# A decoder-layer step in fp32: input and first weight tile in halves, woven; squares of two norms added on VectorE; the root applied to the query tiles

## The reference, cut to what matters

```python
def decoder_layer(x, ...):
    y, ... = head_group_mixer(rms_norm(x, g_mix), ...)    # xn @ w_in (1024 -> 2048), convs, RG-LRU scan, @ w_out
    x = x + y
    x = x + cross_attention(rms_norm(x, g_xa), mem_k, mem_v, w_q, w_o)
    x = x + routed_experts(rms_norm(x, g_moe), moe_w)     # top 4 of 32 experts
    return x, ...
def rms_norm(x, g):
    return x * rsqrt(mean(x * x, axis=-1) + EPS) * g
def cross_attention(xn, k, v, w_q, w_o):
    q = xn @ w_q                                           # 4 heads of 256
    p = softmax(einsum('bthd,bmhd->bhtm', q, k) * 256 ** -0.5)
    return einsum('bhtm,bmhd->bthd', p, v) @ w_o
```

## Time and profile before

| | |
|---|---|
| time, median of 3 runs | 1243.32 us (1242.83 to 1243.99) |
| span of the profiled execution, first to last instruction | 1243.5 us |
| PE busy | 1161.0 us (93%), 5560 matmuls |
| PE weight loads busy | 569.9 us (46%) |
| DVE busy | 331.2 us (27%) |
| ACT busy | 183.6 us (15%) |
| DMA moved | 457.45 MB, 368 GB/s over the span |

### The profile page before, as it was taken

The page is one execution under the profiler, slowest core; times in us unless marked ns, Lnnn a source line. Parts: engine busy times, 40 slices in busy tenths (PEclk is TensorE's granted clock), DMA queues, the critical chain, the costliest instruction groups (busy, mean ns, idle before and its releaser), DMA issues.

```text
span 1243.5 us, 14380 instructions
## 1 busy us (share of the span) xinstructions
PE 1161.0 (93%) x5560; PEld 569.9 (46%) x5560; DVE 331.2 (27%) x799; ACT 183.6 (15%) x357; POOL 44.2 (4%) x86
## 2 busy tenths in 40 slices
PE   8999999998999999999989898989898989999896
PEld 6887888687343343334333333423232323333332
DVE  3795522615212122021212121221202021212113
ACT  3114212303010111111010101011010101010102
POOL 4100001200000000000000000000000000000000
PEclk9999999888899999999999999999999999999999
DMA  9389333994899999999999999999999999999993
GB/s 301 99 273 302 114 127 120 327 420 173 335 427 427 428 429 427 427 429 427 427 428 428 428 428 428 428 428 429 427 428 427 428 428 428 428 428 429 426 426 151
DMA packets 65577, 457.45 MB, mean 368 GB/s; under 512 B 5491, under 2 KB 34379, under 8 KB 40837
## 3 DMA queue, kind: packets, MB, share of 16 engines
q1 hardware_dynamic: 62576, 452.00, 88.5%
q10 hardware_dynamic: 1117, 3.04, 0.7%
q0 software_dynamic: 1856, 2.02, 0.6%
HBM read 453.71 MB, written 3.81 MB: 368 GB/s over the span
## 4 chain that ended last, share of the span: by engine, by line
DMA 48%; PE 45%; DVE 4%; ACT 1%; issue 1%; ACTq 0%; SPq 0%; POOL 0%; DVEq 0%
DMA ring<-in_w_e 47%; PE ps L1625 17%; PE ps L1320 12%; PE ps L1644 5%; PE ps L1339 3%; DVE ring L1009 2%; PE ps L1601 1%; PE ps L1592 1%; PE ps L1546 1%; PE ps L1267 1%; PE ps L1505 1%; PE ps L1256 1%; PE ps L1261 0%; PE ps L1634 0%; PE ps L1454 0%
## 5 line engine op out<-in xcount | busy, mean ns | idle before, releaser
L1625 PE MATMUL ps<-ring,mixed 128*64 128x512 f32 x1536 | 346.8, 596 | 39.6 <-DMA ring<-in_w_e 38.5
L1644 PE MATMUL ps<-ring,mixed 128*64 128x512 f32 x1024 | 229.2, 600 | 0.7 <-issue 0.7
L1625 PEld LDWEIGHTS ps<-ring,mixed 128*64 128x64 f32 x1536 | 105.1, 137 | 265.6 <-issue 182.8
L1161 DVE TENSOR_SCALAR mixed<-ps 128x512 f32<-128x512 f32 x32 | 22.1, 691 | 592.4 <-PE ps L1625 592.4
L1644 PEld LDWEIGHTS ps<-ring,mixed 128*64 128x64 f32 x1024 | 71.6, 138 | 156.2 <-issue 144.0
L733 ACT ACTIVATE mixed<-mixed 128x512 f32<-128x512 f32 x32 | 20.2, 630 | 521.6 <-DVE mixed L1161 521.6
L1601 PEld LDWEIGHTS ps<-mixed 128*128 128x128 f32 x512 | 64.9, 202 | 25.8 <-issue 24.3
L1601 PE MATMUL ps<-mixed 128*128 128x128 f32 x512 | 70.8, 294 | 1.3 <-ACT rstd L715 1.3
L743 ACT ACTIVATE mixed<-ps 64x512 f32<-64x512 f32 x64 | 37.8, 591 | 228.7 <-PE ps L1644 228.3
L1625 PE MATMUL ps<-mixed 128*64 128x512 f32 x256 | 58.2, 596 | 9.3 <-DMA mixed<-in_w_e 9.3
L1320 PE MATMUL ps<-mixed,ring 128*128 128x264 f32 x256 | 60.4, 401 | 0.3 <-ACT mixed L686 0.3
(11 more groups left out here) (305 smaller groups left out, 801.8 us busy)
## 6 DMA issues: line engine op xcount, KB each, us to landing
ring<-in_w_e SPq DMA_DIRECT2D x160, 2048.0 KB, 23.4
low<-in_w_e SPq DMA_DIRECT2D x15, 2048.0 KB, 27.5
mixed<-in_w_e SPq DMA_DIRECT2D x15, 2048.0 KB, 31.8
ring<-in_w_in SPq DMA_DIRECT2D x8, 1024.0 KB, 15.3
ring<-in_cache_mem_k SPq DMA_DIRECT2D x8, 1024.0 KB, 4.9
ring<-in_cache_mem_v SPq DMA_DIRECT2D x8, 1024.0 KB, 8.4
ring<-in_w_k SPq DMA_DIRECT2D x4, 1024.0 KB, 8.8
ring<-in_w_v SPq DMA_DIRECT2D x4, 1024.0 KB, 12.4
```

What stands on the lines that cost most here:

```text
L1161: dve.tensor_scalar(g1, ps[0][:, :], LIMIT, None, ALU.min).then_inc(S["g_clamped"], 1)
L1625: m = pe.matmul(ps[gu][CAP * i:CAP * i + CAP, :], xeT[:, k, CAP * e2:CAP * e2 + CAP], w[:, D * gu + 512 * i:D * gu + 512 * i + 512], start ...
L1644: m = pe.matmul(ps[3][CAP * i:CAP * i + CAP, :], hTv[:, k % 4, CAP * (k // 4):CAP * (k // 4) + CAP], ring[:, s, D * (k % 2) + 512 * i:D * ...
```

## The change

The input's second half is issued after the first half of the first weight tile, and the tile's other half after that. PE first runs 8 matmuls of ones (`WARM`), then transposes and first products woven: four transposed tiles, three products, two tiles, a product, two tiles, four products. DVE and ACT each take four of the tiles out of PSUM, and write `xn` and `xT` both from there. ACT squares four tiles at a time; DVE adds the eight squares in three steps (4, 2 and 1 tiles wide), and `norm_sum` is one matmul, behind output tile 1; the parameters' transposes follow it. Eight of the small parameters' loads move from ACT's queue to the start of POOL's, and POOL's later loads and PE's parameter transposes wait for them too.

For the second norm, DVE writes `xn` = `xT` * gain in the residual loop and adds each square to the sum; PE goes straight on to the query projection, with `norm_sum(1)` (one matmul) behind its first tile; DVE multiplies each query tile by the reciprocal root as it takes it out of PSUM. `kv(6)` is run whole, after the scores. Semaphores that only counted loads are merged, and `sp_turned` becomes the second count of `s_turned`.

```diff
@@ -63,6 +63,7 @@
+WARM = 8
@@ -308,7 +309,7 @@
-n_par = 16 * 12
+n_par, n_more = 16 * len(PAR_ROWS[1::2]), 16 * (len(PAR_ROWS[0::2]) + 2)
@@ -316,7 +317,6 @@
-    sp.dma_start(x0[:, 0:2, 512:D], x_rows[:, :, 512:D]).then_inc(S["xb_loaded"], 16)
@@ -338,7 +338,12 @@
-            sp.dma_start(dst, source(kind, i)).then_inc(filled[n % RING], 16)
+            src = source(kind, i)
+            if kind == "in" and i == 0:
+                sp.dma_start(dst[:, 0:4, :], src[:, 0:4, :]).then_inc(S["in_loaded"], 16)
+                sp.dma_start(x0[:, 0:2, 512:D], x_rows[:, :, 512:D]).then_inc(S["xb_loaded"], 16)
+                dst, src = dst[:, 4:8, :], src[:, 4:8, :]
+            sp.dma_start(dst, src).then_inc(filled[n % RING], 16)
             if kind == "in" and i == 0:
@@ -443,19 +448,24 @@
+    pool.dma_start(stage_a[0:CW * LC, :], a["w_cf_conv"][0].rearrange("w (t c) -> (w t) c", c=P)).then_inc(S["more_loaded"], 16)
+    for r0, rows, src in PAR_ROWS[0::2]:
+        pool.dma_start(stage_b[r0:r0 + rows, :], src).then_inc(S["more_loaded"], 16)
+    pool.dma_start(stage_h, a["state_lru_h"][0]).then_inc(S["more_loaded"], 16)
...
     pool.memset(wgate[:, :, :, :], 0.0).then_inc(S["zeroed"], 1)
...
     pool.wait_ge(S["par_loaded"], n_par)
+    pool.wait_ge(S["more_loaded"], n_more)
@@ -524,20 +534,21 @@
+    act.dma_start(x0[0:NB, 2, :], a["x_sample"].rearrange("b t d -> (b t) d")).then_inc(S["x_loaded"], 16)
...
-    act.dma_start(x0[0:NB, 2, :], a["x_sample"].rearrange("b t d -> (b t) d")).then_inc(S["x_loaded"], 16)
-    act.dma_start(stage_a[0:CW * LC, :], a["w_cf_conv"][0].rearrange("w (t c) -> (w t) c", c=P)).then_inc(S["par_loaded"], 16)
-    for r0, rows, src in PAR_ROWS[0::2]:
-        act.dma_start(stage_b[r0:r0 + rows, :], src).then_inc(S["par_loaded"], 16)
-    act.dma_start(stage_h, a["state_lru_h"][0]).then_inc(S["h0_loaded"], 16)
...
     act.wait_ge(S["consts"], 2)
...
-    for k in range(KD):
-        act.wait_ge(S["x_copied"], k + 1)
-        act.activation(xn[:, k, :], xT[:, k, :], ACT.Copy, scale=par[:, C_GMIX + k:C_GMIX + k + 1]).then_inc(S["xn_ready"], 1)
-        act.activation(sq[:, k, :], xT[:, k, :], ACT.Square).then_inc(S["x_squared"], 1)
+    for k in range(1, KD, 2):
+        src = ps[IN_BANK[k % 4]][:, 0:TOK]
+        act.wait_ge(S["x_turned"], k + 1)
+        act.activation(xn[:, k, :], src, ACT.Copy, scale=par[:, C_GMIX + k:C_GMIX + k + 1]).then_inc(S["xa_kept"], 1)
+        act.activation(xT[:, k, :], src, ACT.Copy).then_inc(S["xa_kept"], 1)
+    for i in range(2):
+        act.wait_ge(S["xd_kept"], 4 * i + 4)
+        act.wait_ge(S["xa_kept"], 4 * i + 4)
+        act.activation(sq[:, 4 * i:4 * i + 4, :], xT[:, 4 * i:4 * i + 4, :], ACT.Square).then_inc(S["x_squared"], 1)
     def root(n):
@@ -633,9 +644,6 @@
-    for o in range(KD):
-        wait_tile(act, "q", "q_done", o)
-        act.activation(qT[:, o, :], ps[o % 4][:, 0:TOK], ACT.Copy, scale=HD ** -0.5).then_inc(S["q_kept"], 1)
...
         act.wait_ge(S["qs_turned"], i + 1)
@@ -802,9 +810,17 @@
-    for k in range(KD):
+    dve.wait_ge(S["gain_ready"], 1)
+    for k in range(0, KD, 2):
+        src = ps[IN_BANK[k % 4]][:, 0:TOK]
...
-        dve.tensor_copy(xT[:, k, :], ps[IN_BANK[k % 4]][:, 0:TOK]).then_inc(S["x_copied"], 1)
+        dve.tensor_scalar(xn[:, k, :], src, par[:, C_GMIX + k:C_GMIX + k + 1], None, ALU.mult).then_inc(S["xd_kept"], 1)
+        dve.tensor_copy(xT[:, k, :], src).then_inc(S["xd_kept"], 1)
...
+    dve.wait_ge(S["x_squared"], 2)
+    for n, w in enumerate((4, 2, 1)):
+        dve.tensor_tensor(sq[:, 0:w, :], sq[:, 0:w, :], sq[:, w:2 * w, :], ALU.add).then_inc(S["sq_added"], 1)
+        dve.wait_ge(S["sq_added"], n + 1)
     dve.wait_ge(S["sd_ready"], 1)
@@ -815,7 +831,8 @@
     keep_za(0)
-    dve.wait_ge(S["xn_ready"], KD)
+    dve.wait_ge(S["xa_kept"], KD)
+    dve.wait_ge(S["xd_kept"], KD)
@@ -833,23 +850,13 @@
-    def norm(n, gain):
...
-        dve.wait_ge(S["sd_ready"], n + 1)
-        dve.reciprocal(rstd[:, :], rstd[:, :]).then_inc(S["rstd_ready"], 1)
-        dve.wait_ge(S["rstd_ready"], n + 1)
-        for k in range(KD):
-            dve.scalar_tensor_tensor(out=xn[:, k, :], in0=xT[:, k, :], scalar=par[:, gain + k:gain + k + 1],
-                                     in1=rstd[:, :], op0=ALU.mult, op1=ALU.mult).then_inc(S["xn_ready"], 1)
@@ -975,18 +982,33 @@
-    def residual(kind, done, base, gain=None):
+    def add_square(k):
...
+        dve.wait_ge(S["x_squared"], 2 + k + 1)
+        dve.wait_ge(S["sq_added"], 3 + k - 1)
+        dve.tensor_tensor(sq[:, 0, :], sq[:, 0, :], sq[:, k, :], ALU.add).then_inc(S["sq_added"], 1)
...
+    def residual(kind, done, base, gain, squares=False):
...
-            if gain is not None:
-                dve.wait_ge(S["res_added"], base + o + 1)
-                dve.tensor_scalar(xn[:, o, :], xT[:, o, :], par[:, gain + o:gain + o + 1], None,
-                                  ALU.mult).then_inc(S["xn_ready"], 1)
+            dve.wait_ge(S["res_added"], base + o + 1)
+            dve.tensor_scalar(xn[:, o, :], xT[:, o, :], par[:, gain + o:gain + o + 1], None,
+                              ALU.mult).then_inc(S["xn_ready"], 1)
+            if squares and o >= 2:
+                add_square(o - 1)
+        if squares:
+            add_square(KD - 1)
...
-    residual("out", "out_done", 0)
-    norm(1, C_GXA)
+    residual("out", "out_done", 0, C_GXA, squares=True)
+    dve.wait_ge(S["sd_ready"], 2)
+    dve.reciprocal(rstd[:, :], rstd[:, :]).then_inc(S["rstd_ready"], 1)
+    dve.wait_ge(S["rstd_ready"], 2)
+    for o in range(KD):
+        wait_tile(dve, "q", "q_done", o)
+        dve.scalar_tensor_tensor(out=qT[:, o, :], in0=ps[o % 4][:, 0:TOK], scalar=HD ** -0.5, in1=rstd[:, :],
+                                 op0=ALU.mult, op1=ALU.mult).then_inc(S["q_kept"], 1)
@@ -1242,40 +1264,62 @@
+    pe.wait_ge(S["consts"], 1)
+    for _ in range(WARM):
+        pe.matmul(ps[6][:, 0:P], ones[:, :], ones[:, :], start=True, stop=True)
...
-    for k in range(KD):
+    def turn_input(k):
...
-            pe.wait_ge(S["x_copied"], k - 3)
+            pe.wait_ge(S["xa_kept" if k % 2 else "xd_kept"], k - k % 2 - 2)
...
-    pe.wait_ge(filled[START["in"] % RING], 16 * fills_before(START["in"]))
-    for k in range(KD):
-        pe.wait_ge(S["xn_ready"], k + 1)
...
+    def first_product(k):
...
+        if k == 0:
+            pe.wait_ge(S["in_loaded"], 16)
+        if k == 4:
+            pe.wait_ge(filled[START["in"] % RING], 16 * fills_before(START["in"]))
+        pe.wait_ge(S["xa_kept" if k % 2 else "xd_kept"], k - k % 2 + 1)
...
-    m.then_inc(S["in_done"], 1)
+        if k == KD - 1:
+            m.then_inc(S["in_done"], 1)
...
+    for k in range(4):
+        turn_input(k)
+    for k in range(3):
+        first_product(k)
+    turn_input(4)
+    turn_input(5)
+    first_product(3)
+    turn_input(6)
+    turn_input(7)
+    for k in range(4, KD):
+        first_product(k)
+    pe.wait_ge(S["xd_kept"], KD)
+    pe.wait_ge(S["xa_kept"], KD)
...
     def norm_sum(n):
...
-        for k in range(KD):
-            pe.wait_ge(S["x_squared"], KD * n + k + 1)
-            m = pe.matmul(ps[5][:, 0:TOK], ones[:, :], sq[:, k, :], start=(k == 0), stop=(k == KD - 1))
-        m.then_inc(S["sum_done"], 1)
...
-    pe.wait_ge(S["consts"], 2)
-    norm_sum(0)
-    pe.wait_ge(S["par_loaded"], n_par)
-    pe.wait_ge(S["h0_loaded"], 16)
-    pe.transpose(ps[4][:, 0:C_B], stage_a[0:C_B, :], ident[0:C_B, 0:C_B])
-    pe.transpose(ps[4][:, C_B:C_GMIX], stage_b[0:B_ROWS, :], ident[0:B_ROWS, 0:B_ROWS])
-    for c in range(LC):
-        m = pe.transpose(ps[4][:, C_H0 + NB * c:C_H0 + NB * c + NB], stage_h[:, c * P:(c + 1) * P], ident[0:NB, 0:NB])
-    m.then_inc(S["par_turned"], 1)
+        pe.wait_ge(S["sq_added"], (3, 3 + KD - 1)[n])
+        pe.matmul(ps[5][:, 0:TOK], ones[:, :], sq[:, 0, :], start=True, stop=True).then_inc(S["sum_done"], 1)
...
+    def turn_params():
+        pe.wait_ge(S["par_loaded"], n_par)
+        pe.wait_ge(S["more_loaded"], n_more)
+        pe.transpose(ps[4][:, 0:C_B], stage_a[0:C_B, :], ident[0:C_B, 0:C_B])
+        pe.transpose(ps[4][:, C_B:C_GMIX], stage_b[0:B_ROWS, :], ident[0:B_ROWS, 0:B_ROWS])
+        for c in range(LC):
+            m = pe.transpose(ps[4][:, C_H0 + NB * c:C_H0 + NB * c + NB], stage_h[:, c * P:(c + 1) * P], ident[0:NB, 0:NB])
+        m.then_inc(S["par_turned"], 1)
@@ -1321,6 +1365,11 @@
                 m.then_inc(S["freed" if half else done], 1)
+                if kind == "in" and o == 1:
+                    norm_sum(0)
+                    turn_params()
+                if kind == "q" and o == 0:
+                    norm_sum(1)
@@ -1407,10 +1456,6 @@
-    norm_sum(1)
...
-    pe.wait_ge(S["rows_kept"], 1)
-    kv(6, (0,))
@@ -1418,7 +1463,7 @@
-    project("q", "q_done", lambda k: xn[:, k, :], q_free, lambda k: pe.wait_ge(S["xn_ready"], KD + k + 1))
```

(22 more changed lines are left out.)

## The result

| | before | after |
|---|---|---|
| median of 5 executions, us | 1243.99 (1242.83 to 1244.72) | 1239.01 (1233.77 to 1239.16) |
| profiled execution: time, span, us | about 1245.1 (see below); 1243.5 | 1239.16; 1237.6 |

The ratio is 0.995, interval 0.994 to 0.996: 5.0 us gained where 12.4 were forecast. The time lies 1.0 us above the range (1228 to 1238), 1.6 above the figure of rival B (1237.4) and 8.0 above that of A (1231); 0.7 of it is that before itself has 1243.99 here and had 1243.32 in the forecast. An execution takes 1.6 us more than its span (1239.16 against 1237.6), so that of before took about 1245.1; the forecast had taken its span, 1243.5, as its time.

The account below looks back on a forecast made before the run. The expert-weight stream sets the pace, its start set by PE's path before the first expert. First stage 7.8 plus second norm net 4.6 gave 12.4 us off 1243.5: 1231 us, range 1228 to 1238.

Parts of the forecast that it names:

- rival B: Clock stays low in the first stage, which gains 1.3 us instead of 7.8: 1237.4 us; 35% with halfway cases.
- A: The forecast itself, first products at full clock: 1231 us, within 1228.5 to 1233; 55%.
- I take it that they do: Program start: assumes about 3 us of ones' matmuls lift PE's clock before the first products, though no row shows it.
- Loads bind at full clock: First stage: x and weight halves landing at 7.0, 9.1 and 11.2 pace PE; products end at 13.0, not 18.21.
- POOL's eight loads cost nothing: Parameter loads moved to POOL's start all land by 13, before PE asks at 17.4; cover 4 us.
- rival D: POOL's parameter loads come late and hold PE, making the kernel slower, 1246 us; 7% with mishaps of its size.
- Second norm, 6.56 us out of the path: Ahead of the query projection: sum of eight and half of kv(6) leave, one matmul returns; 6.56 us saved.
- 2.0 back behind the scores: Half of kv(6), 3.45 us, returns behind the scores; 2.0 us taken as showing, bounds 0 and 3.45; net gain 4.6.
- (b): Last slot of cached values comes up to 3.45 us later, at 244.95, so PE reads it 1.4 us late.
- (a): DVE's copy of the last sample token's scores has 1.0 us of cover, so 2.45 of the 3.45 us show.
- One for one to the end: Expert-weight stream restarts when PE frees slots, so PE time saved before the first expert comes off the end fully.
- Rival C: No change: the expert-weight stream starts when loads allow, not PE, and takes the gain back; 1243 us, 3%.

Follow-up runs that it names:

- e3: Changed kernel without the 8 matmuls of ones (WARM = 0): 1236.72 us, ratio 0.9934 to the kernel before.
- e10: Changed kernel without the 8 matmuls of ones, run again: 1236.23 us, ratio 0.9934 to the kernel before.
- e9: The changed kernel itself, run again: 1238.44 us, ratio 0.9947 to the kernel before; its profiled execution took 1233.74.
- e1: Changed kernel's first stage with the second norm as in the kernel before: 1240.13 us (12 executions), ratio 0.9964.
- e8: One more execution of the kernel with the changed first stage alone, second norm as before: 1240.62 us.
- e2: Kernel before with the second norm's change alone: 1239.48 us (7 executions), ratio 0.9971.
- e11: Changed kernel with memory-token transposes and small cache products spread between input projection tiles instead of one burst: 1230.41 us, ratio 0.9894.
- e4: Changed kernel with 16 matmuls of ones instead of 8: 1236.49 us, ratio 0.9937 to the kernel before.
- e6: Changed kernel with 16 matmuls of ones and the store of mem_v issued later: 1235.53 us, ratio 0.9937 to the kernel before.
- e12: Changed kernel with spread transposes, 16 matmuls of ones and the late mem_v store together: 1234.83 us, ratio 0.9928 to the kernel before.

## Why the prediction was wrong

The step that failed is "I take it that they do": that the ones' matmuls lift the clock. On it rested 6.5 of the first stage's 7.8 us (25.2 against rival B's 31.7). In the profiled execution the clock stayed low until the products were over, tile 4 gained 1.4, and `kv` nothing. Three findings carry this. (1) With 0 ones, 12 executions of e3 and e10 took 1233.0 to 1234.6 (six) and 1238.0 to 1239.8 (six); with 8, the changed kernel's 11 took 1231.3 to 1233.8 (three) and 1238.2 to 1239.8 (eight). Taking the ones away doesn't make the kernel measurably slower. (2) The same kernel ran case A (e9, 1233.74) and case B (first profile, 1239.16), so the forecast's sum for the first stage was right to 0.1 us, and its condition holds in some executions only. (3) e1, with the first stage alone, fell into two groups 6.9 us apart in the mean, near the 6.5 between the cases. The forecast asked "does it rise?" for a thing that this program does not settle. Where the clock falls later counts as well: e8 and e10 had an early first stage and lost much of it again.

Going through the other steps:

- *Loads bind at full clock.* Failed, and luck hid it. Tile 1 starts at 13.47 in e9, forecast 13.0, and the sum follows at 17.03; but PE had no gap from 5.36 on. The last weight half landed at 10.0 in e9 and 10.2 in the first profile (forecast 11.2), before its products. The forecast priced the work too low: its transposes, 2.84 us by the earlier trace rows, took 3.95, and the eight products 4.15 instead of 3.56. A wait that never came and work that took longer cancel to 0.5 us.
- *POOL's eight loads cost nothing* (rival D's ground): held. They were issued from 1.54 on, POOL's next step behind their landing started at 11.6, and PE asked at 23.5.
- *Second norm, 6.56 us out of the path*: held, 6.5.
- *2.0 back behind the scores*: from the query projection's end to the `o` projection's start before took 50.3 us; e2 took 51.7 (248.31 - 196.65), e11 51.8, the changed kernel 53.0, e9 53.3, e10 54.9. So 1.4 where the clock stayed up, which is (b) to the tenth, and 2.7 to 4.6 where it was low around 230. The 2.0 lies between. Both (a) and (b) were there: in e2 DVE's copy waits 1.75 us for PE, and PE then 1.4 for the cached values. It is (b) that ends last there, and the forecast had put (a) first. That before too was at the low level there, from 232.0 to 238.8, makes its 50.3 no clean base.
- *One for one to the end*: held in every trace, 934.0 to 934.6 us from the first expert product to the end. Rival C is out.
- *Nothing between `o` and the first expert*: not seen at all. The changed kernel gained 2.2 us there (3.7 to 5.9), 1.6 of it in the `o` projection (30.23 against 31.82), by less low clock: 10.2 us between 249 us and the first expert product, before 17.1 from 252 to 307. So the 5.9 us of the profile are not rival B's 4.6 plus 1.3, though the sum is alike, and that is luck: 3.7 from the norm, 0 from the first stage, 2.2 from where the clock happened to be low.

The range had B's figure in it and still ended 1.0 us too low. B's 35% was too small: in before the products took 6.20 us where 3.56 is the price at the high level, so they had run for some 5.3 us (twice the difference, an estimate) before it rose, longer than the 3.8 us of the ones. That should have put B ahead of A; the forecast's "some 3 us of it earlier" has no row behind it. It had also named a clock that falls again inside the woven stage. That came in e8 (8.3 to 11.7 us) and not in e4, e6, e9, e11 and e12; what set it off is open. The low level at 64 us followed a burst of transposes and tiny matmuls. The Trainium skill (TensorE: Matmul & The Clock Gate, Part 4: PE-mode transpose), by which transposes don't count as busy in the same way, is in keeping with that; no run here separates the transposes from the small matmuls beside them.

Open: what settles in one execution whether the clock rises at 5, at 12 or at 20 us, and where it falls later; what the late store is worth; why e11 is faster by more than the 0.9 us at `kv`.

## What to carry over

Where an edit's gain is a clock level, ask whether every execution takes it: with 16 ones all three traces had their products at 386 ns from the first, with 8 or none the nine traces of this stage went every way, with medians from 386 to 647. And count what the remedy costs: the 16 ones put the transposes off by 1.4 to 2.1 us. And look for the places where the level falls. Here a burst of transposes and tiny matmuls came before the one near 65 us; taking it apart made the kernel 6 to 8 us faster, of which the traces explain 0.9 by a wait that went away and leave the rest with the clock, cause open. Take several executions before you read a difference of 5 us, and a profile only beside its own time: it is one draw.

## What was not expected of the hardware

The granted clock falls to 0.50 four to six times before 345 us, 24 to 38 us in all, at different places in executions of one kernel, and the time follows: 1231.3 to 1239.8 us for the changed kernel, where the kernel before stays within 1242.3 to 1246.1. And the granted clock of a row can mislead at the start: it read 1.00 from 0 to 20 us in the changed kernel while each product took 647 ns, and 1.00 also in e9 with the same products at 386. There only the durations tell the level. The row of the changed kernel for 9 to 12 us, granted clock third from the end:

```profile
9.00:12.00 3.00, 3.00 (x8) 2.01 (x7) 0.00 (x0) 0.57 (x2) 0.39 (x1) 1.00 1.03 383
```
